# A two-block transformer on one core: high and low hidden activations side by side, and one 512-column matmul past each high weight in the 256-token down-projections

## The reference

```
def swiglu(x, w_gate, w_up, w_down):
    return (jax.nn.silu(x @ w_gate) * (x @ w_up)) @ w_down
# first block, each of 2 layers
h = layer_norm(ALPHA * h + 0.5 * swiglu(h, ...), ...)
h = layer_norm(ALPHA * h + mix, ln2_g[l], ln2_b[l])
h = layer_norm(ALPHA * h + 0.5 * swiglu(h, ...), ...)
# second block, each of 2 layers
x = x + 0.5 * swiglu_2(rmsnorm(x, ffn1_norm[l]), ...)
x = x + y          # mixer: pooling, Fourier, differential attention, then w_out
x = x + 0.5 * swiglu_2(rmsnorm(x, ffn2_norm[l]), ...)
# at the end: rmsnorm(x, final_norm)
```

## Time and profile before

| | us |
|---|---|
| median of 3 runs | 1962.82 (1962.23 to 1964.01) |
| the profiled execution, its own time | 1963.27 |
| its span, first to last instruction | 1961.5 |
| PE busy in the span | 1943.2 (99%) |
| DVE busy | 1428.9 (73%) |
| ACT busy | 1019.7 (52%) |
| POOL busy | 152.7 (8%) |
| mean DMA rate | 177 GB/s |

### The profile page before, as it was taken

The page is one execution under the profiler, slowest core; times in us unless marked ns, Lnnn a source line. Parts: engine busy times, 40 slices in busy tenths (PEclk is TensorE's granted clock), DMA queues, the critical chain, the costliest instruction groups (busy, mean ns, idle before and its releaser), DMA issues.

```text
span 1961.5 us, 42313 instructions
## 1 busy us (share of the span) xinstructions
PE 1943.2 (99%) x16150; PEld 1901.9 (97%) x16150; DVE 1428.9 (73%) x2593; ACT 1019.7 (52%) x1525; POOL 152.7 (8%) x192
## 2 busy tenths in 40 slices
PE   9999999999999999999999999999999999999998
PEld 8999989999999999899999999999999999989998
DVE  6774787987588768879878775667765775667763
ACT  4443687554455446865446443565445444465443
POOL 0001123000100011320010100000000000100000
PEclk9999999999999999999999999999999999999999
DMA  7454433445454544345553665435565555435554
GB/s 263 171 198 166 165 108 122 179 171 190 154 187 172 185 173 148 109 151 194 203 182 130 229 234 193 151 133 190 192 220 176 193 200 207 150 130 188 194 215 153
DMA packets 46830, 346.66 MB, mean 177 GB/s; under 512 B 5344, under 2 KB 6416, under 8 KB 9232
## 3 DMA queue, kind: packets, MB, share of 16 engines
q1 hardware_dynamic: 44416, 335.63, 47.6%
q0 software_dynamic: 2320, 9.74, 1.6%
HBM read 344.29 MB, written 1.07 MB: 176 GB/s over the span
## 4 chain that ended last, share of the span: by engine, by line
PE 80%; issue 9%; DVE 6%; ACT 2%; DVEq 1%; DMA 1%; POOL 1%; POOLq 0%; ACTq 0%; SPq 0%
PE ps L591 26%; PE ps L592 26%; PE ps L593 26%; DVE w_lo L1911 1%; ACT w_hi L1237 1%; DMA raw<-in_w_up 1%; POOLq L2797 0%; DVE pj L2359 0%; DVE cst L2380 0%; DVE pj L2356 0%; ACT scratch L1588 0%; DVE scratch L2325 0%; PE ps L927 0%; PE ps L938 0%; DVE plain L2022 0%
## 5 line engine op out<-in xcount | busy, mean ns | idle before, releaser
L1911 DVE TENSOR_TENSOR w_lo<-raw,w_hi 128x1024 fp32r<-128x1024 f32 (+1 forms) x582 | 748.7, 1313 | 167.9 <-ACT w_hi L1237 165.8
L1237 ACT ACTIVATE w_hi<-raw 128x1024 fp32r<-128x1024 f32 (+1 forms) x582 | 635.1, 1122 | 121.1 <-PE ps L593 103.2
L591 PE MATMUL ps<-x_hi,w_lo 128*128 128x256 f32 (+3 forms) x2416 | 685.7, 284 | 3.8 <-DVE x_lo L1998 1.4
L592 PE MATMUL ps<-x_lo,w_hi 128*128 128x256 f32 (+3 forms) x2416 | 676.0, 280 | 0.0
L593 PE MATMUL ps<-x_hi,w_hi 128*128 128x256 f32 (+3 forms) x2416 | 675.4, 280 | 0.0
L591 PEld LDWEIGHTS ps<-x_hi,w_lo 128*128 128x128 f32 x2416 | 454.6, 188 | 12.7 <-issue 6.8
L592 PEld LDWEIGHTS ps<-x_lo,w_hi 128*128 128x128 f32 x2416 | 454.1, 188 | 0.8
L593 PEld LDWEIGHTS ps<-x_hi,w_hi 128*128 128x128 f32 x2416 | 454.6, 188 | 0.0
L591 PE MATMUL ps<-hid_hi,w_lo 128*128 128x256 f32 (+1 forms) x1536 | 431.9, 281 | 0.8 <-DVE hid_lo L2109 0.5
L593 PE MATMUL ps<-hid_hi,w_hi 128*128 128x256 f32 (+1 forms) x1536 | 430.2, 280 | 0.0
L592 PE MATMUL ps<-hid_lo,w_hi 128*128 128x256 f32 (+1 forms) x1536 | 429.9, 280 | 0.0
(11 more groups left out here) (330 smaller groups left out, 1555.5 us busy)
## 6 DMA issues: line engine op xcount, KB each, us to landing
raw<-in_w_up SPq DMA_DIRECT2D x176, 1024.0 KB, 4.8
raw<-in_w_down SPq DMA_DIRECT2D x64, 1408.0 KB, 6.0
raw<-in_w_in SPq DMA_DIRECT2D x36, 1024.0 KB, 4.8
raw<-in_w_out SPq DMA_DIRECT2D x16, 1024.0 KB, 4.8
cst<-row_copy POOLq DMA_DIRECT2D x2, 1088.0 KB, 8.4
raw<-in_w_up SPq DMA_DIRECT2D x4, 512.0 KB, 6.9
cst<-in_consts POOLq DMA_DIRECT2D x1, 1537.5 KB, 7.2
prm<-in_prm POOLq DMA_DIRECT2D x2, 690.0 KB, 7.5
```

What stands on the lines that cost most here:

```text
L591: mm(dst, w_lo[:, j, cols], xa, start=first, stop=False)
L592: mm(dst, w_hi[:, j, cols], xb, start=False, stop=False)
L1237: fn(w_hi[:, j, c], raw[:, j, c], ACT.Copy).then_inc(hi_done, 1)
L1911: v.tensor_tensor(w_lo[:, j, c], raw[:, j, c], w_hi[:, j, c].bitcast(F32), ALU.subtract)\
```

## The change

The high and low hidden activations lie in one buffer `hid`. For 256 tokens, `hid_both` has chunk f as 512 columns, 256 high and then 256 low, from column 48 + 512 f. For 272 tokens the two parts stand apart as before. The high weight passes all 512 columns in one matmul into a whole PSUM bank, so that the bank's left half gets high x high and the right half high x low; the low weight passes the 256 high columns into the left half. At the last step the two stand in the other order. VectorE adds both halves of the bank to `h`: two operations per chunk with a drain between them (`resid_halves`, and a second one in `level_down`), and the semaphore is raised by the second. Scratch views in the same memory move along. In the diff, the views `early`, `y_squares` and `used[0]` are such.

```
-        HID_HI_T2, HID_LO_T2 = 3 * LINE, LINE
-        hid_hi_all = sb("hid_hi", [P, HID_HI_W], F32R)
-        hid_lo_all = sb("hid_lo", [P, HID_LO_W], F32R)
+        HID_HI_W, HID_LO_W, HID_T2 = NF * T1 + 4 * LINE, NF * T1, 3 * LINE
+        hid = sb("hid", [P, HID_HI_W + HID_LO_W], F32R)
...
+        hid_both = chunks(hid[:, HID_T2:], NF, 2 * T2)
+        hidt_hi, hidt_lo = hid_both[:, :, 0:T2], hid_both[:, :, T2:2 * T2]
...
                             for c in range(HALF_F):
...
-                                last = three(ps[:, 4 + j, 0:T], j, slice(col, col + P),
-                                             ha[:, f, 0:T], hb[:, f, 0:T], f == 0, f == NF - 1)
+                                if T == T2:
+                                    if f < NF - 1:
+                                        mm(ps[:, 4 + j, :], w_hi[:, j, col:col + P], hid_both[:, f, :], start=f == 0, stop=False)
+                                    last = mm(ps[:, 4 + j, 0:T2], w_lo[:, j, col:col + P], ha[:, f, :], start=False, stop=False)
+                                    if f == NF - 1:
+                                        last = mm(ps[:, 4 + j, :], w_hi[:, j, col:col + P], hid_both[:, f, :],
+                                                  start=False, stop=True)
+                                else:
+                                    last = three(...)
...
+            def resid_halves(m, bank):
+                c = slice(m, m + 1) if isinstance(m, int) else bass.ds(m, 1)
+                dst = h[:, c, T1 - T2:T1]
+                v.tensor_tensor(dst, dst, ps[:, bank:bank + 1, 0:T2], ALU.add)
+                dve.drain()
+                v.tensor_tensor(dst, dst, ps[:, bank:bank + 1, T2:2 * T2], ALU.add).then_inc(resid_ready, 1)
...
-                    v.scalar_tensor_tensor(out=c, in0=ps[:, 4 + m % 2, 0:T], scalar=0.5, in1=c,
-                                           op0=ALU.mult, op1=ALU.add).then_inc(resid_ready, 1)
+                    last = v.scalar_tensor_tensor(out=c, in0=ps[:, 4 + m % 2, 0:T], scalar=0.5, in1=c, op0=ALU.mult, op1=ALU.add)
+                    if T == T2:
+                        dve.drain()
+                        last = v.scalar_tensor_tensor(out=c, in0=ps[:, 4 + m % 2, T2:2 * T2], scalar=0.5, in1=c,
+                                                      op0=ALU.mult, op1=ALU.add)
+                    last.then_inc(resid_ready, 1)
...
-                        resid(alpha, it * 2 + j, 4 + j, T)
+                        resid_halves(it * 2 + j, 4 + j)
...
-                        resid(1.0, it * 2 + j, 4 + j, T2)
+                        resid_halves(it * 2 + j, 4 + j)
```

More of the change, by code:

```diff
@@ L232, in build @@
         small = sb("small", [P, 96])
-        HID_HI_W, HID_LO_W = NF * T1 + 4 * LINE, NF * T1 + LINE
-        HID_HI_T2, HID_LO_T2 = 3 * LINE, LINE
-        hid_hi_all = sb("hid_hi", [P, HID_HI_W], F32R)
-        hid_lo_all = sb("hid_lo", [P, HID_LO_W], F32R)
+        HID_HI_W, HID_LO_W, HID_T2 = NF * T1 + 4 * LINE, NF * T1, 3 * LINE
+        hid = sb("hid", [P, HID_HI_W + HID_LO_W], F32R)
         SCRATCH = HID_HI_W + HID_LO_W
@@ L266, in build @@
         xt_hi, xt_lo = chunks(x_hi_all, KD, T2), chunks(x_lo_all, KD, T2)
-        hid_hi, hid_lo = chunks(hid_hi_all, NF, T1), chunks(hid_lo_all, NF, T1)
-        hidt_hi, hidt_lo = chunks(hid_hi_all[:, HID_HI_T2:], NF, T2), chunks(hid_lo_all[:, HID_LO_T2:], NF, T2)
+        hid_hi, hid_lo = chunks(hid, NF, T1), chunks(hid[:, HID_HI_W:], NF, T1)
+        hid_both = chunks(hid[:, HID_T2:], NF, 2 * T2)
+        hidt_hi, hidt_lo = hid_both[:, :, 0:T2], hid_both[:, :, T2:2 * T2]
         plain_hi, plain_lo = (chunks(plain[:, i * PLAIN_HALF:i * PLAIN_HALF + KD * X_PITCH], KD, X_PITCH) for i in range(2))
@@ L452, in build @@
         assert CC_FIRST + (SSD_HEADS + 2) * S_W <= CC_W
-        used[0] = HID_HI_T2 + KD * T2
+        used[0] = HID_T2 + KD * 2 * T2
         cat_hi2, cat_lo2 = hidt_hi[:, 0:KD, :], hidt_lo[:, 0:KD, :]
-        early = [scr[:, at + KD // 2 * T2 + 512 * i:at + KD // 2 * T2 + 512 * (i + 1)]
-                 for at in (HID_HI_T2, HID_HI_W + HID_LO_T2) for i in range(2)]
+        early = [scr[:, HID_T2 + 2 * T2 * k:HID_T2 + 2 * T2 * (k + 1)] for k in range(KD // 2, KD)]
         fold = early[0].rearrange("p (e c t) -> p e c t", e=2, c=2)
@@ L464, in build @@
         atok = take(2, T2)
-        used[0] = HID_HI_W + HID_LO_T2 + KD * T2
         vtok = take(2, 512)
@@ L469, in build @@
         poolm = take(2, T2)
-        y_squares = scr[:, HID_HI_T2 + 14 * T2:HID_HI_T2 + 22 * T2].rearrange("p (k t) -> p k t", k=KD)
+        y_squares = scr[:, HID_T2 + (2 * NF - KD) * T2:HID_T2 + 2 * NF * T2].rearrange("p (k t) -> p k t", k=KD)
         def plain_par(name, k=0, n=1):
@@ L766, in turn @@
                                 col = u * W_WIDE + c * P
-                                last = three(ps[:, 4 + j, 0:T], j, slice(col, col + P),
-                                             ha[:, f, 0:T], hb[:, f, 0:T], f == 0, f == NF - 1)
+                                if T == T2:
[6 more added lines that the diff above has]
+                                else:
+                                    last = three(ps[:, 4 + j, 0:T], j, slice(col, col + P),
+                                                 ha[:, f, 0:T], hb[:, f, 0:T], f == 0, f == NF - 1)
                             last.then_inc(unit_used, 1)
```

## The result

| | before | after |
|---|---|---|
| median of the runs on one chip | 1962.76 us (4 runs) | 1974.91 us (4 runs, 1974.29 to 1976.52) |
| ratio | | 1.0063 [1.0051, 1.0076] |
| span of the profiled execution | 1961.5 us | 1972.7 us |
| granted clock, mean | 0.999 | 0.999 |
| one step (a 128 x 128 weight tile), steady | 340.0 ns | 353.3 ns |

The changed kernel is slower by 0.6%, 12.2 us by the medians and 11.2 by the spans. The forecast was 1959.1 us, faster, and its range ended at 1961.6.

A forecast was written before the change was run, and what follows sets the result against it. TensorE was taken to bound the kernel, at 113.3 ns a matmul in the 256-token down-projections. -4.69 + 0.48 + 0.50 = -3.7 us, laid on the 1962.8 median, gave 1959.1 us, range 1955.1 to 1961.6.

The forecast's parts named there:

- The bound and the count: 256-token down-projections: TensorE busy all through; five of 176 steps change, 880, while the output projections keep three matmuls.
- The step that failed: 256-token down-projections: a 512-column matmul costs 220.0 ns, a step 333.3, 6.67 less; -4.69 us in block two; chance 0.66.
- `level_down`: First 256-token down-projection: VectorE gets nearly full, so the point where TensorE waits for `x_lo` moves by +0.48 us.
- the tail: Behind the last down-projection: nothing hides VectorE's second add, plus 0.50 us.
- The float32 records: Full float32 matmuls: 110 ns at 128 columns, 215 at 256, 2 to 3 ns over at either length; lower bound 328.3 a step.
- The 120 ns of 258 columns: 258-column matmuls: 12.5 ns over their columns, read as fitting neither a share of the columns nor a floor under every matmul.
- rival D: 256-token down-projections: the 512-column read meets the weight load, 5 ns in each matmul, 343.3 ns a step, 1967.2 us; chance 0.08.
- Chunks start at the same column modulo 128 as before: 256-token down-projections: the pairs of buffers read together, moving column block and weights loaded beside it, remain.
- Rival C: 256-token down-projections: the cost goes with the columns, a step stays 340.0 ns, +1.5, 1964.3 us; chance 0.11.
- Rival B: 256-token down-projections: weight load sets the pace, a long matmul hides it; 328.3 ns a step, -7.2, 1955.6 us; chance 0.15.
- VectorE's terms: One more drained operation per chunk, about 0.50 us: free inside block two, +0.48 in the first down-projection, +0.50 at the end.
- 2.0 us of room: Behind the three down-projections that `down` makes: `x_lo` of the last k has 2.0 us spare, 1.2 go, nothing lost.

The follow-up runs named there:

- the tails: Changed kernel plus groups of further matmuls on TensorE behind the last mean square, writing no output, with chunk places, weight places and widths varied; the first took 2173.43 us.
- the shifted place: Changed kernel with its hidden chunks 16 columns later (HID_T2 of 4 lines in place of 3): 1971.14 us, ratio to the kernel before 1.0039.
- s = 4: Group in the first probe behind the changed kernel, hidden chunks starting at column 16 s of `hid` + 512 f: 512 columns alone took 228.5 ns.

## Why the prediction was wrong

**The bound and the count were right.** TensorE sets the time, 880 steps changed, and inside a down-projection nothing waits that did not wait before.

**The step that failed** is the one under the words "6.67 ns for each matmul whatever its length, 213.3 + 6.7 = 220.0 ns, a step 333.3 ns". The long matmul takes 233.3 ns, 20 over its columns, and the short one, which the sum left at 113.3, takes 120.0. Instead of -6.67 ns a step it was +13.3 when steady. Over 176 steps that was -1.17 us forecast against +2.10 measured, four times in block two: 4 x 3.27 = 13.1 us of the 15.8 between the forecast and the result. `level_down` has another 2.2 (2.65 where 0.48 was expected). These two make 15.3; the tail was right. By the spans of the two profiled executions the miss is 14.9 (11.2 measured, -3.7 forecast), and what the stretches outside the change differ by (-1.01 and +0.48) is most of the rest.

Why the reasoning missed it:
- It took the earlier trace rows's 113.3 ns for a constant of the instruction. It is the price at the best of the places; moved by 16 columns, the same kernel pays 119.1 on the mean. The 6.67 ns did not have to be divided between a matmul and its columns: the rest could get worse.
- The float32 records of the earlier trace rows are another kind of matmul. One float32 matmul of the program makes two records with a weight load each (L1137 runs twice and leaves the four of the row), and each takes about twice the time of its columns, as the prediction noticed itself. They said nothing of a float32r matmul with a load beside it, though both kinds were called a matmul of so many columns.
- The 120 ns of 258 columns and the 125 of 272 were the rows that spoke of stalls. The prediction read the first as evidence for its own case, and used the second only in rival D.
- "Chunks start at the same column modulo 128 as before" was true, and beside the point. The place that was good for three reads of 256 columns and their weights is not good for one of 512 and one of 256 with the same weight tiles.

**Rival D** had the right sign, and its name, a long read that meets the weight load, is the reading that the runs leave as the likeliest. Its ground was wrong: it put the 125.0 ns of 272 columns down to chunks that start at changing places, but in the tails, where the chunks start at the same place in every step, three of 272 columns take 373.3 ns at the least, 124.4 each. Its size was too small: 13.3 ns more a step were measured where it had 3.3, 353.3 and not 343.3 ns. The sign that it named, a long matmul of some 229 ns, came as 233.3. What was put against D, that the chunks' places don't change from step to step, does not tell a good place from a bad one, and its chance of 0.08 rested on it.

**Rival C**, the cost goes with the columns, is what holds at the best places: 226.8 ns is twice 113.3, and the pair is worth exactly the three matmuls. At such a place the change would by this have been C's case; no kernel was built there. What C's time would be can be read off the kernel with three matmuls in the new layout, whose step is 340.0: +2.4 us by the medians, 1.8 of them at VectorE's places, where C gave +1.5. Rival B is half right in that a floor of 112 ns exists, close to 113.3. A long matmul gains nothing by lying over it, since its own excess is larger, 13.4 ns at the best place against 6.7.

The Trainium skill (TensorE: Matmul & The Clock Gate, section Back-to-back issue gap) gives an isolated matmul N / 2.4 + 2.5 ns, 215.8 for 512 columns, and a sustained spacing of about 131 ns for 512 columns. The runs agree with neither for 512 columns of float32r: the lowest mean of a long matmul in any group of the tails is 225.4 ns.

**VectorE's terms were right**: the second half 0.50 us behind the first, the loop of 7.25 us in `level_down`, +0.50 in the tail (0.49 measured), two halves of 0.50 in the chain behind the seventh chunk (1.00 measured), no wait at `lo_done` or `resid_ready`, and nothing lost behind the three down-projections that `down` makes, where 2.0 us of room had been found. That VectorE would set the pace of `level_down` held for two chunks only, since TensorE was slower than foreseen.

**What stays open.** Shown is that the price depends on the places of both the moving operand (in a period of 64 columns) and the weights, and neither on VectorE, nor on DMAs, nor on the PSUM bank, at a granted clock of 1.00. That the two reads hold each other up in the memory is the likeliest reading of this, and only argued. The opening and the stretches from 735 to 985 us differ by up to 1.2 us between kernels of this study whose code is the same there. The largest of these is a change of spacing: the 1056 matmuls of 258 columns ahead of `level_down` follow at 120.0 ns in seven of the nine traces and at 121.1 in two (three matmuls in the new layout, and the kernel before moved by 16 columns), 1.2 us in all. The cause wasn't tried, and executions of one kernel differ by as much (the kernel before took 1962.1 to 1964.5 us), so it need not be the kernels'. What the pair at the shifted place owes its 347 ns in the kernel and 350 in the tail to is open as well. The changed kernel with its low-weight tiles moved to a pairing of 340 ns wasn't built. By the tails it would at most draw level on TensorE and still have VectorE's second add to pay. No version that beats the kernel before was found.

## What to carry to other kernels

A measured spacing of matmuls is the price of a shape at a place; before fewer and longer matmuls are counted as a gain, the new shape has to be timed, in a tail behind the kernel if need be, with both operands where they will lie. Where matmuls and weight loads run back to back, moving a buffer by 16 columns can be worth more than the change of instructions: here 16 us for the kernel before. And where a row shows a neighbouring shape with a cost that doesn't fit the model (258 columns at 120 ns), that row says how far the model can be wrong, upwards too.

## What the runs showed of the hardware

- A float32r matmul with a weight load of 128 columns beside it took 111.6 to 111.8 ns for 64, 128 and 192 columns alike, at the one place tried.
- The excess over the columns grows with the length: 11.1 ns at 256 columns, 13.3 at 320, 14.8 at 384, 15.6 at 448, 20.2 at 512, all at one place; 6.7 for 256 and 13.4 for 512 columns at the best places.
- The price has a period of 64 columns (256 bytes a partition) in where the moving operand starts: a settled group and the one 64 columns later agree to 0.5 ns. It also depends on where the weight tile starts. Of 64 pairings, 6 took 340.0 ns a step and the others 346.5 to 353.5, many of them at 346.7, 350.0 or 353.3.
- The spacing needs time to settle: in the changed kernel the first five steps of a chunk take 345 to 354 ns and 347.6 on the mean, and only then 353.3; a row of 512-column matmuls at s = 4 went from up to 236 ns to a steady 226.7 only behind its tenth.
